# Memory attention with exponentials by query tile, and four smaller changes at phase borders, in a one-core inference step

## The reference, cut to what matters

```python
def _mem_attention(q, mk, mv):
    ...
    logits = jnp.einsum('blhd,bhmd->bhlm', q, mk.astype(q.dtype)).astype(jnp.float32) * (MEM_DH ** -0.5)
    p = jax.nn.softmax(logits, axis=-1).astype(q.dtype)
    return jnp.einsum('bhlm,bhmd->blhd', p, mv.astype(q.dtype)).reshape(B, L, MEM_HEADS * MEM_DH)

def _hgrn_chunk(s0, q, k, logf, v):
    b = jnp.cumsum(logf, axis=2)
    ...
    decay = jnp.exp(jnp.where(causal, b[:, :, :, None, :] - b[:, :, None, :, :], -jnp.inf))
    scores = jnp.einsum('bhtsd,bhsd->bhts', decay * q[:, :, :, None, :], k)
    o = (jnp.einsum('bhts,bhsv->bhtv', scores, v)
         + jnp.einsum('bhtd,bhdv->bhtv', q * jnp.exp(b), s0))
    ...

def _layer(...):
    h = _rmsnorm(x, norm_attn)
    ...
    x = x + _merge(ya, yb, yc, gl, w_branch, w_out)
    f, conv_new = _conv_ffn(_rmsnorm(x, norm_ffn), conv_prev, w_up, conv_w, conv_b, w_down)
```

## Time and profile before

| | us |
|---|---|
| median of 3 runs (3280.57 to 3289.64) | 3284.94 |
| the profiled execution's own time | 3285.09 |
| its span, first to last instruction | 3283.3 |
| TensorE matmuls busy | 3127.9 (95%) |
| TensorE weight loads busy | 2946.4 (90%) |
| VectorE busy | 1384.2 (42%) |
| ScalarE busy | 1131.1 (34%) |
| GpSimd busy | 862.8 (26%) |

### The profile page before, as it was taken

How to read it: one execution, slowest core, us unless ns; L and a number is a source line. 1 busy time by engine, 2 the same in 40 slices (tenths; PEclk the granted TensorE clock), 3 DMA queues, 4 the chain that set the end, 5 groups by cost and what they waited for, 6 DMA issues and landing times. The chain is left out here.

```text
span 3283.3 us, 50029 instructions
## 1 busy us (share of the span) xinstructions
PE 3127.9 (95%) x19550; PEld 2946.4 (90%) x19550; DVE 1384.2 (42%) x1453; ACT 1131.1 (34%) x1594; POOL 862.8 (26%) x515
## 2 busy tenths in 40 slices
PE   7899999999999999999688989999989999999997
PEld 6899999999988888888477879999979999999996
DVE  5554444544335555555432331222044444444443
ACT  5244433444234444444332330222142222222222
POOL 2333233332211211212002221334323222222220
PEclk9999999999999999999899999999989999999998
DMA  5311221121258776877756654432211111111101
GB/s 148 92 53 54 61 66 54 46 68 54 61 113 156 142 115 141 154 133 145 132 116 158 148 180 143 147 103 74 67 58 45 38 45 38 45 38 38 38 26 69
DMA packets 684752, 295.69 MB, mean 90 GB/s; under 512 B 350524, under 2 KB 665436, under 8 KB 684680
## 3 DMA queue, kind: packets, MB, share of 16 engines
q1 hardware_dynamic: 680232, 285.90, 36.2%
q10 hardware_dynamic: 4448, 8.80, 0.7%
HBM read 240.23 MB, written 54.41 MB: 90 GB/s over the span
## 5 line engine op out<-in xcount | busy, mean ns | idle before, releaser
L119 POOL TENSOR_TENSOR weight_lo<-weight_stage,weight_hi 128x1024 fp32r<-128x1024 f32 x180 | 457.5, 2542 | 1365.1 <-ACT weight_hi L114 1364.9
L1939 PE MATMUL group<-h_hi_part,weight_hi 128*128 128x384 f32 x1056 | 359.8, 341 | 12.6 <-POOL weight_lo L119 7.9
L166 PE MATMUL group<-h_hi_part,weight_hi 128*128 128x384 f32 x984 | 348.9, 355 | 17.7 <-DVE key_rows L727 5.2
L1940 PE MATMUL group<-h_lo_part,weight_hi 128*128 128x384 f32 x1056 | 359.5, 340 | 0.0
L1941 PE MATMUL group<-h_hi_part,weight_lo 128*128 128x384 f32 x1056 | 359.3, 340 | 0.0
L114 ACT ACTIVATE weight_hi<-weight_stage 128x1024 fp32r<-128x1024 f32 x180 | 190.9, 1061 | 417.9 <-PE group L2206 244.0
L167 PE MATMUL group<-h_lo_part,weight_hi 128*128 128x384 f32 x984 | 334.0, 339 | 0.0
L168 PE MATMUL group<-h_hi_part,weight_lo 128*128 128x384 f32 x984 | 333.9, 339 | 0.0
L2204 PE MATMUL group<-h_hi_part,weight_hi 128*128 128x384 f32 x768 | 259.7, 338 | 7.2 <-PEq L1551 7.2
L2205 PE MATMUL group<-h_lo_part,weight_hi 128*128 128x384 f32 x768 | 258.8, 337 | 0.0
L2206 PE MATMUL group<-h_hi_part,weight_lo 128*128 128x384 f32 x768 | 258.8, 337 | 0.0
(11 more groups left out here) (352 smaller groups left out, 6570.7 us busy)
## 6 DMA issues: line engine op xcount, KB each, us to landing
weight_stage<-in_w_in SPq DMA_DIRECT2D x88, 512.0 KB, 4.8
cached_v<-in_cache_diff_v SPq DMA_DIRECT2D x128, 256.0 KB, 5.0
cached_k<-in_cache_diff_k SPq DMA_DIRECT2D x224, 128.0 KB, 4.2
weight_stage<-in_w_up SPq DMA_DIRECT2D x44, 512.0 KB, 3.9
gate_in<-scratch_gates SPq DMA_DIRECT2D x24, 576.0 KB, 3.8
weight_stage<-in_w_branch SPq DMA_DIRECT2D x24, 512.0 KB, 4.0
down_stage<-in_w_down SPq DMA_DIRECT2D x22, 512.0 KB, 3.6
scratch_gates<-gate SPq DMA_DIRECT2D x16, 576.0 KB, 4.1
```

The lines of the kernel that those rows point to most:

```text
L119: pool.tensor_tensor(self.wlo[:, n % 2, :], self.wst[:, n % 2, :], self.whi[:, n % 2, :].bitcast(F32), ALU.subtract).then_inc(self.w_lo, 1)
L166: pe.matmul(out, wh[:, k, :], xh[:, k, cols], start=(k == 0), stop=False)
L1939: pe.matmul(o, w[0][:, k, :], ahi[:, k, rows], start=(k == 0), stop=False)
L1940: pe.matmul(o, w[0][:, k, :], alo[:, k, rows], start=False, stop=False)
```

## The change

Five edits.

1. Memory attention, S: VectorE takes the row maximum and negates it; ScalarE takes eight exponentials of 128x256, one for each query tile, with the negated maximum as bias and the row sum as a second result; VectorE inverts the sums and scales. The subtraction in PSUM and the reduction for the sums are gone. The sample scores SL are as before.
2. HGRN, level 6: the product is taken of 64 by 64 columns, into PSUM rows 0 to 63 and columns 64 to 127 of each tile.
3. Differential attention: TensorE's wait for the constants stands in `sample_columns`.
4. Border of memory attention and merge: eight buffers for the first branch's tiles (two more in the parts of the memory tokens, three in `cached_mem_v`); loads 3 and 4 wait for the last head's value product, 5 to 7 for its sample product; the roundings of tiles 6 and 7 stand between the copies of O0 and O1.
5. Border of merge and FFN: the last 36 matmuls of V0 stand in the FFN's block, ahead of G1.

```diff
+                def last_level():
+                    n, half = f"L{LEVELS - 1}", P // 2
+                    x = xx[(LEVELS - 1) % 2]
+                    ps, _ = take(n)
+                    pe.wait_ge(xr_r, i * LEVELS + LEVELS)
+                    pe.wait_ge(xl_r, i * LEVELS + LEVELS)
+                    for t in range(PT):
+                        left, right = t * P, t * P + half
+                        col = (t % TPC) * P + half
+                        last = pe.matmul(ps[0:half, t // TPC, col:col + half], x[:, left:left + half],
+                                         x[:, right:right + half], start=True, stop=True)
+                    last.then_inc(g.full, 1)
+
                 def level(l):
+                    if l == LEVELS - 1:
+                        return last_level()
...
                 def sample_columns(n):
                     ps = take(f"OC{n}")
                     R.wait_freed(pe, f"OS{n}", i)
+                    pe.wait_ge(consts_in, cb + 64)
...
-            pe.wait_ge(consts_in, cb + 64)
             with pe.Fori(0, HEADS - 1) as i:
                 head(i)
...
-    y0 = [flat(kc[:].rearrange("p b m n -> p b (m n)"))[:, n * ROWS:(n + 1) * ROWS] for n in range(3)]
+    y0 = [flat(t[:].rearrange("p b m n -> p b (m n)"))[:, n * ROWS:(n + 1) * ROWS] for t in (kc, vc) for n in range(3)]
+    y0[3:3] = [flat(t[:].bitcast(F32))[:, 0:ROWS] for t in (mhi, mlo)]
...
             def load_y0(k):
-                if k >= 3:
-                    sp.wait_ge(g.ylo_r, k - 2)
-                sp.dma_start(y0[k % 3], g.s["y_branch"][0, k]).then_inc(g.y_in[k], 16)
+                if k == 3:
+                    sp.wait_ge(g.full, last_R.full_value("V", 0))
+                elif k == 5:
+                    sp.wait_ge(g.full, last_R.full_value("OS", 0))
+                sp.dma_start(y0[k], g.s["y_branch"][0, k]).then_inc(g.y_in[k], 16)
...
                 act.wait_ge(shift_r, i + 1)
                 ps = R.ready(act, "S", r)
-                finish("S", act.activation(flat(pr[:]), flat(ps), ACT.Exp))
+                s_rows = flat(ps).rearrange("p (t n) -> p t n", n=MEM)
+                for t in range(PT):
+                    ins = act.activation(pr[:, t, :], s_rows[:, t, :], ACT.Exp, bias=mx[:, t:t + 1],
+                                         accum_out=sm[:, t:t + 1])
+                finish("S", ins)
...
                     finish(f"O{c}", act.activation(yc[:, c, 0:SEQ], flat(ps[:, 0:2, :]), ACT.Copy))
+                    if last and c == 0:
+                        for k in range(6, KT):
+                            y0_hi(k)
...
             head(MH - 1, last=True)
-            for k in range(6, KT):
-                y0_hi(k)
...
-                shift("S", PT, mx, shift_r)
+                ps = R.ready(dve, "S", r)
+                g.dve.done(dve.tensor_reduce(mx[:], flat(ps).rearrange("p (t n) -> p t n", n=MEM), AX.X, ALU.max))
+                dve.tensor_scalar(mx[:], mx[:], -1.0, None, ALU.mult).then_inc(shift_r, 1)
                 if last:
                     y0_lo(0)
-                normalize("S", PT, pr[:], sm, probs_r)
+                R.wait_freed(dve, "S", r)
+                g.dve.done(dve.reciprocal(sm[:], sm[:]))
+                dve.tensor_tensor(pr[:], pr[:], sm[:].unsqueeze(2).to_broadcast([P, PT, MEM]), ALU.mult)\
+                    .then_inc(probs_r, 1)
...
                 pe.wait_ge(h_lo, k + 1)
                 last = up_step(pe, *first[0], ahi, alo, k)
             last.then_inc(g.full, 1)
-            for k in range(KT // 2, KT):
-                last = up_step(pe, *first[1], ahi, alo, k)
-            last.then_inc(g.full, 1)
...
             for j, name in enumerate(("G0", "V0", "G1", "V1")):
-                if j >= 2:
+                if j == 1:
+                    ps, w = g.psum[(head.base + head.k[name]) % 2], g.w_parts(pe, j)
+                    for k in range(KT // 2, KT):
+                        last = up_step(pe, ps, w, ahi, alo, k)
+                    last.then_inc(g.full, 1)
+                elif j:
                     up(head, name, 0, j, 0)
```

More of the change, by code:

```diff
@@ L1642, in y0_hi @@
                 act.wait_ge(g.y_in[k], 16)
-                act.activation(g.hhi[:, k, :], y0[k % 3], ACT.Copy).then_inc(g.yhi_r, 1)
+                act.activation(g.hhi[:, k, :], y0[k], ACT.Copy).then_inc(g.yhi_r, 1)
             def head(i, last=False):
@@ L1749, in y0_lo @@
                 dve.wait_ge(g.yhi_r, k + 1)
-                dve.tensor_tensor(g.hlo[:, k, :], y0[k % 3], g.hhi[:, k, :].bitcast(F32), ALU.subtract)\
+                dve.tensor_tensor(g.hlo[:, k, :], y0[k], g.hhi[:, k, :].bitcast(F32), ALU.subtract)\
                     .then_inc(g.ylo_r, 1)
@@ L1784, in _ @@
             with dve.Fori(0, MH - 1) as i:
-                g.dve.loop(i, 6)
+                g.dve.loop(i, 5)
                 head(i)
```

## The result

The changed kernel takes 3253.5 us (median of four runs, 3248.9 to 3257.8) against 3287.3 us before (four runs, 3280.6 to 3291.3): a ratio of 0.991, 95% interval 0.989 to 0.992. The forecast was 3251, range 3242 to 3264. The execution profiled after took 3249.8 us, of which 3248.0 are span; before, the span was 3283.3.

The account below looks back on a forecast made before the run. TensorE, busy 95% of the span, was taken to bound the kernel, so only fewer instructions or shorter waits help. Terms 7.0 + 4.6 + 6.7 + 8.4 + 7.2 = 33.9 off 3285.1 gave 3251 us, range 3242 to 3264.

Parts of the forecast that it names:

- Quarter blocks, -7.0: HGRN level 6: 128 matmul instructions on 64x64 instead of 128x128 blocks save 55 ns each, -7.0 us.
- Both of the forecast's limits: HGRN level 6: weight load (116 ns) and column stream (120 ns) each stand at the matmul pitch; the change halves both.
- nothing else moves: HGRN level 6: eight 128x128 products per head become eight 64x64 ones, with no other change counted in the -7.0 us.
- The slower rival: HGRN level 6: narrow loads not hidden, 357 ns an instruction, +30.2 us, 3288; loses from 206 ns more each; chance 0.03.
- Start of the differential attention, -4.6: TensorE's 7.1 us constants wait leaves the start; second score product starts at about 937.0 instead of 941.64, -4.6 us.
- the named chain: Differential attention start: VectorE's constants wait, then ScalarE's value copy and first exponentials, free the second score product's bank at 936.93.
- the condition: Differential attention start: if the clock falls in the shorter wait, 24 matmuls take 0.32 each and the gain is about 3.
- First three memory heads, -6.7: Memory attention: exponentials by query tile shorten waits by 0.6, 2.25 and 2.25 us, plus 1.6 from the clock, -6.7 us.
- Last head and merge border, -8.4: Last head -2.3; border wait 7.2 to 2.1 via output copy, store issue, crossing, -5.1; clock -1.0; in all -8.4 us.
- The late-loads rival: Merge border: five transfers at once land near 1955, some 3 us lost, 3254; chance 0.09.
- FFN border, -7.2: 36 matmuls moved across run beside the weight load, -6.2 us, wait of about 1.0 left; clock 1.0 more, -7.2 us.
- their two terms (9.0): Memory attention exponentials: 6.7 us in the first three heads and 2.3 us in the last head.

Follow-up runs that it names:

- widths_in_turn: Changed kernel, but every second quarter block loads all 128 columns as weights, so the weight width changes inside each group; 3264.2 us.
- value_before: Changed kernel with all of the first value product ahead of the border to the FFN again; 3262.3 us.
- second profile: The changed kernel itself measured and profiled once more, with no edit; 3255.4 us, ratio 0.991 to before.
- one_exp: Changed kernel with the memory attention's exponentials in one instruction again, subtraction and row sums back on VectorE; 3265.9 us.
- value_middle: Changed kernel with 45 instead of 36 matmuls of the first value product moved across the FFN border; 3253.8 us.
- value_later: Changed kernel with 54 instead of 36 matmuls of the first value product moved across the FFN border; 3254.0 us.
- three_y: Changed kernel with three buffers for the first branch's blocks and the late rounding again, as before; 3261.4 us.

## Why the prediction was right, point by point

The sum was 33.9 us; the two profiled spans differ by 35.3, the medians by 33.8, and by 28.3 in the second measurement. So the agreement to a tenth is luck, and the sum is right partly because misses cancelled: the quarter blocks and the FFN border gave less than forecast, the exponentials more.

1. **Quarter blocks, -7.0: mis-sized, -3.2 to -3.8.** Both of the forecast's limits showed, and its saving on a block was right: it took the spacing from 121 to 66 ns, the traces have 112 and 58, so 54 ns are saved and not 55 (the 121 is the mean busy time of the earlier trace rows, which is more than the spacing). The step that failed is "nothing else moves": the term priced the blocks and not the ends of a group, where a load of another width is not made behind the running matmul; that took 0.35 us in each head, 2.8 in all. That leaves 4.1 (8 heads by 0.51); the few tenths to the stage's difference weren't traced. The slower rival (every load exposed) has its mechanism in the idle 0.25 us, but only where the width changes: widths_in_turn, with 8 changes a group, is the nearest to it, 157 ns a block (2.51 us for 16). The prediction's break-even of this rival has a slip: 26.9 us over 128 instructions are 210 ns, not 206; nothing hangs on it. Of the rule of the Trainium skill that the prediction named (TensorE: Matmul & The Clock Gate, section Part 3: Packing small matmuls — row/col tiling), the trace agrees with the exception, the background buffer: within a group of one width the 138 ns loads are hidden at 58 ns a block.

2. **Start of the differential attention, -4.6: right, -4.1 to -5.7 in the two profiles (-5.3 in the mean of eleven), by the named chain.** TensorE stops 2.15 us for the query blocks, as forecast. Its second score product came at 10.5 us, with 11 expected. The clock did fall in this shorter wait, as the condition said (0.72 of 2.4 GHz over the 24 matmuls), so that they took 5.7 us from the first start to the last; but since the chain over VectorE's constants and ScalarE's exponentials sets the second score product, at its start TensorE waited only 0.63 us for it, and the slow matmuls lay inside that chain. Two other profiles bear this out: in value_before and widths_in_turn the clock didn't fall after the same wait, the 24 matmuls took 4.1 us, and the stage took 765.1 and 764.4, no less than the others. The condition's "about 3" was too low for that reason.

The start and what released it, changed kernel:

```profile
923.53 0.49 PE L1415 MATMUL group<-diff_k,diff_q 64*128 64x128 f32 x4 [2.15 <-POOL query_blocks L1348]
...
928.76 0.20 ACT L1124 ACTIVATE row_max<-row_max 128x2 f32<-128x2 f32 x1 [14.69 <-DVE row_max L1253]
...
931.87 0.70 PE L1415 MATMUL group<-diff_k,diff_q 64*128 64x256 f32 x4 [0.63 <-ACT probs L1159]
```

3. **First three memory heads, -6.7: right in the chain, one head mis-sized; -6.4 and -10.7 in the two profiles.** Heads come every 59.2 to 59.4 us instead of 61.4 to 62.9 (62.0 for the first distance of the second profile). The second and third head give about 2.0 each, with 2.25 forecast. For the first the forecast had only 0.6, since a copy of the sample rows would hold TensorE behind the transposes; there the wait left was 0.21 us, and 0.03 in the second profile, so this head gives about 2 as well:

```profile
1744.36 1.97 PE L1918 MATMUL group<-ident,mem_probs 128*128 128x128 f32 x16
1746.54 0.63 PE L1924 MATMUL group<-ident,sample_probs 128*128 128x128 f32 x4 [0.21 <-ACT sample_probs L1707]
```

ScalarE made that copy sooner, because it stood idle ahead of it, issuing stores, for 1.62 us and not for the 2.97 of the earlier trace rows. The clock's part was put at 1.6 in all and varies. A wait of the first head for the transposed keys (1.6 us after, 4.5 in the second profile, 3.8 before) varies from run to run, with and without the edit, and with it the stage; 2.2 us of the -10.7 are this wait and not the edit.

4. **Last head and merge border, -8.4: -7.3 and up to -1.9 from the clock (a few tenths in the second profile), near the term.** The wait left is 2.23 us, 2.1 forecast, but not by the chain that was named (fence above): VectorE's last remainder ends at 1935.14, behind ScalarE's copy (1934.44) and the store's issue (1934.85), and the crossing takes 0.48 from there, as in the earlier trace rows. The late-loads rival didn't come about: ScalarE waited 0.75 us for one load, and not at all for the two tiles between the output copies. The price by edit was off on both sides: the buffers 3.6 us of wait rather than 5.1, since part of the old wait went with the faster last head, and the exponentials 4.0 (one_exp, 33.7 against 29.7) rather than 2.3.

5. **FFN border, -7.2: short, -5.2, with 1.4 behind it that the second profile doesn't show.** The 6.2 us of work moved and ran beside the load as forecast. The wait left was 2.1, not 1.0: the weight landed 5.0 us after its issue instead of 4.1.

```profile
2388.73 5.02 DMA weight_stage<-in_w_up
2393.77 1.07 ACT weight_hi L114
2394.91 2.36 POOL weight_lo L119
2397.32 0.44 PE group L1967
```

That is the changed kernel's chain of waits at this border. The same transfer took 5.0 to 5.5 us in all nine profiles in which 36 matmuls are moved, and 4.0 to 4.1 in the four others (before, value_before, value_middle, value_later). So it goes with where the border lies, and not with matmuls running beside it as such, since they run beside it with 45 and 54 too. What makes it slower wasn't found.

Undone one at a time, the edits cost 11.4 (exponentials), 7.8 (FFN border), 6.9 (buffers) and 3.7 us (constants) against 3254.5, the middle of the changed kernel's two medians, and the quarter blocks 3.5 by their stage: 33.3 us, about the whole difference of the first measurement. So no overlap of the edits shows, within an error of several us: each of the four medians is of runs that spread by 5 to 7 us, and the FFN border has 7.8 here and 5.0 in its stage. The exponentials are worth more than their two terms (9.0) gave them.

## What to carry to other kernels

Where a wait ends a chain of passes over a whole tile, the cheapest cut is a pass that another engine can give as a by-product (here the row sums and the shift within the exponentials): only what leaves the chain ahead of the last wait counts, and the time to spare behind it has to be read from the trace. Work that is moved across a border to cover a load has a best amount, set by the next thing that is late on either side; two runs with different amounts find it. When a matmul is made smaller, price both its sides and also the first and last of its group, since a change of width is not free.

## What was not expected of the hardware

- Load and stream each hold f32 matmuls of 128 columns about as far apart as both together (112 ns): with half the stream they start 112 ns apart, with half the load 109, with half of both 58.
- A group of 16 matmuls with 64-column weights between products with 128-column weights costs about 0.35 us at its ends (0.25 of it seen as idle time of the first narrow load), and 0.14 us for each change of width inside it.
- The same wait of 2.2 us at the merge border is followed by the full clock in eight of eleven executions (1.00 in the changed kernel) and by a stretch partly at the lower level in three (0.61 in the second profile, above), worth 1.6 us, while 2.15 us at the start of the differential attention are followed by such a stretch in nine of eleven; after 5.9 us (three_y) it was 0.50. What decides it after the short waits stays open.
